# Feed-forward of a two-block kernel: weight split ahead of the conv tap, a narrower bank wait, two tiles of the second down product moved forward

## The reference, cut to what matters

```
h = rmsnorm_2(x, ffn_norm_g[l])
u = causal_dwconv(h @ w_up[l], conv_w[l], conv_b[l])
gate, val = jnp.split(u, 2, axis=-1)
x = x + (jax.nn.silu(gate) * val) @ w_down[l]
```

## Time and profile before

| | |
|---|---|
| median of 3 runs | 2674.45 us (2674.26 to 2674.68) |
| the profiled execution's own time | 2673.48 us |
| its span in the trace | 2671.7 us |
| PE busy | 2590.9 us, 97% of the span |
| DVE, ACT, POOL busy | 1443.6, 973.5, 795.2 us |
| mean granted TensorE clock | 0.993 of full |

### The profile page before, as it was taken

How to read it: one execution, slowest core, us unless ns; L and a number is a source line. 1 busy time by engine, 2 the same in 40 slices (tenths; PEclk the granted TensorE clock), 3 DMA queues, 4 the chain that set the end, 5 groups by cost and what they waited for, 6 DMA issues and landing times. The chain is left out here.

```text
span 2671.7 us, 32450 instructions
## 1 busy us (share of the span) xinstructions
PE 2590.9 (97%) x12954; PEld 2147.6 (80%) x12954; DVE 1443.6 (54%) x1290; ACT 973.5 (36%) x1380; POOL 795.2 (30%) x318
## 2 busy tenths in 40 slices
PE   7999999999999999999999999989999999999999
PEld 3788888888788888888788888877778788878887
DVE  4674546565666753444735355456866515641664
ACT  3420034435344430023556555564144302221234
POOL 2565453333443335542111011011412222222230
PEclk9999999999999999999999999999999999999999
DMA  7232221212222154241011011031111111112111
GB/s 314 73 107 69 91 84 55 61 63 64 68 71 68 48 193 139 94 142 64 32 40 40 32 40 38 34 124 51 48 39 47 48 49 46 51 51 63 47 55 63
DMA packets 55896, 194.20 MB, mean 73 GB/s; under 512 B 6584, under 2 KB 10296, under 8 KB 54624
## 3 DMA queue, kind: packets, MB, share of 16 engines
q1 hardware_dynamic: 40656, 141.61, 16.0%
q10 hardware_dynamic: 15120, 50.90, 5.4%
HBM read 158.36 MB, written 29.92 MB: 70 GB/s over the span
## 5 line engine op out<-in xcount | busy, mean ns | idle before, releaser
L238 PE MATMUL G<-H_hi,w_hi 128*128 128x512 f32 x1648 | 514.4, 393 | 7.7 <-POOL w_lo L269 4.9
L269 POOL TENSOR_TENSOR w_lo<-w_raw,w_hi 128x1024 fp32r<-128x1024 f32 x133 | 361.9, 2721 | 498.1 <-ACT w_hi L263 492.3
L238 PE MATMUL G<-H_lo,w_hi 128*128 128x512 f32 x1648 | 508.7, 390 | 0.0
L238 PE MATMUL G<-H_hi,w_lo 128*128 128x512 f32 x1648 | 508.2, 390 | 0.0
L264 POOL TENSOR_TENSOR w_hi<-w_raw,ones 128x1024 fp32r<-128x1024 f32 x75 | 195.4, 2606 | 647.0 <-PE G L238 489.9
L238 PEld LDWEIGHTS G<-H_hi,w_hi 128*128 128x128 f32 x1648 | 307.3, 188 | 73.9 <-issue 11.1
L238 PEld LDWEIGHTS G<-H_lo,w_hi 128*128 128x128 f32 x1648 | 309.9, 188 | 65.1
L238 PEld LDWEIGHTS G<-H_hi,w_lo 128*128 128x128 f32 x1648 | 309.9, 188 | 64.8
L1774 POOL TENSOR_TENSOR w_lo<-w_raw,w_hi 128x1024 fp32r<-128x1024 f32 x24 | 60.1, 2506 | 493.6 <-ACT w_hi L1983 493.6
L1824 PE MATMUL G<-A_hi,w_hi 128*128 128x512 f32 x368 | 156.9, 426 | 15.5 <-DVE projected L2166 15.2
L1876 PEld LDWEIGHTS G<-att_v,probsT 128*128 128x128 f32 x1152 | 147.9, 193 | 24.4 <-ACT probsT L2012 15.3
(11 more groups left out here) (497 smaller groups left out, 4549.1 us busy)
## 6 DMA issues: line engine op xcount, KB each, us to landing
w_raw<-w_in SPq DMA_DIRECT2D x65, 512.0 KB, 3.6
w_raw<-w_up SPq DMA_DIRECT2D x44, 512.0 KB, 3.6
pre_raw<-w_in SPq DMA_DIRECT2D x30, 512.0 KB, 3.6
w_raw<-w_out SPq DMA_DIRECT2D x16, 512.0 KB, 3.6
w_raw<-w_down SPq DMA_DIRECT2D x16, 512.0 KB, 3.6
wm<-w_mod SPq DMA_DIRECT2D x6, 1024.0 KB, 16.9
xT<-xT SPq DMA_DIRECT2D x8, 512.0 KB, 19.1
wm<-w_mod SPq DMA_DIRECT2D x2, 2048.0 KB, 24.2
```

What stands on the lines that cost most here:

```text
L238: mm = nc.tensor.matmul(dst[:, n * NB:n * NB + c], w[:, k, :], m[:, k, n * NB:n * NB + c], start=first, stop=last)
L269: nc.gpsimd.tensor_tensor(w_lo[:, slot, 0:kt, :], w_raw[:, slot, 0:kt, :], w_hi[:, slot, 0:kt, :].bitcast(F32), ALU.subtract).then_inc(w_r ...
```

## The change

Three edits in the feed-forward.

1. The first up product (job 135, `G[1]`) waits for `out2 early` number 6, the last reader of `G[1]`, and no longer for `out2 late` number 7, which reads `G[0]`. The second keeps the old wait. Both still wait for the last `out2 lo` ahead of their last k-tile.
2. `next_high` stands at the start of each half turn on ACT, ahead of the wait for `normed` and the tap.
3. In groups 0 and 1, down product 0 does all k-tiles but the last, then product 1 its first two, then product 0 its last (with the wait for `lo`), then product 1 the rest. Products 2 to 7 are as before.

```diff
@@ -2382,7 +2382,8 @@
                     if g == 0:
                         if m == 0:
                             S.wait(pe, "dve", "out2 lo", KT - 2)
-                        gemm(up + m, (up + m) % 2, H, ("dve", "out2 late", KT - 1), late=("dve", "out2 lo", KT - 1))
+                        gemm(up + m, (up + m) % 2, H, ("dve", "out2 late", KT - 1) if m else ("dve", "out2 early", KT - 2),
+                             late=("dve", "out2 lo", KT - 1))
@@ -2396,8 +2397,25 @@
                 if g < LAST:
                     S.wait(pe, "dve", f"up{g} lo", nf - 2)
-                    products_of_8(f"down{g}", down, A, nf, late=("dve", f"up{g} lo", nf - 1),
-                                  freed=[("dve", f"up{g} normed {m}", nf - 1) for m in range(2)])
+                    for m, tiles in ((0, range(nf - 1)), (1, range(2)), (0, range(nf - 1, nf)), (1, range(2, nf))):
+                        if tiles[0] == 0:
+                            pe.wait_ge(w_ready, down + m + 1)
+                            S.wait(pe, "dve", f"up{g} normed {m}", nf - 1)
+                        if tiles[-1] == nf - 1:
+                            S.wait(pe, "dve", f"up{g} lo", nf - 1)
+                        slot = (down + m) % 2
+                        for k in tiles:
+                            for w, mov in ((w_hi, A[0]), (w_hi, A[1]), (w_lo, A[0])):
+                                for n in range(2):
+                                    mm = pe.matmul(G[slot][:, halves[n]], w[:, slot, k, :], mov[:, k, halves[n]],
+                                                   start=k == 0 and w is w_hi and mov is A[0], stop=k == nf - 1 and w is w_lo)
+                        if tiles[-1] == nf - 1:
+                            mm.then_inc(gemm_done, 1)
@@ -2488,10 +2506,10 @@
                     for m in range(2):
+                        next_high(up, f, m)
                         S.wait(act, "dve", f"up{g} normed {m}", f)
                         settle(act, f)
                         tap(f"up{g}", m, f + (f0 + m * FT))
-                        next_high(up, f, m)
```

More of the change, by code:

```diff
@@ L2398, in _ @@
                     S.wait(pe, "dve", f"up{g} lo", nf - 2)
-                    products_of_8(f"down{g}", down, A, nf, late=("dve", f"up{g} lo", nf - 1),
-                                  freed=[("dve", f"up{g} normed {m}", nf - 1) for m in range(2)])
+                    for m, tiles in ((0, range(nf - 1)), (1, range(2)), (0, range(nf - 1, nf)), (1, range(2, nf))):
[12 more added lines that the diff above has]
+                            mm.then_inc(gemm_done, 1)
+                    S.enter("pe", f"down{g}")
+                    with pe.Fori(1, KT // 2) as i:
+                        for m in range(2):
+                            gemm(down + 2 * i + m, (down + m) % 2, A, ("dve", f"down{g} job {m}", i - 1), kt=nf, pair=G[(down + m) % 2])
+                    S.leave("pe", KT // 2)
             gemm(down - 2, up % 2, H, ("dve", f"up{LAST} normed 0", LAST_F - 1))
```

## The result

| | before | changed |
|---|---|---|
| median of 5 runs | 2674.45 us | 2658.86 us |
| the profiled execution's own time | 2673.48 us | 2659.00 us |
| span of it | 2671.7 us | 2657.2 us |
| PE busy | 2590.9 us | 2586.2 us |
| mean granted clock | 0.993 | 0.995 |

The changed kernel is faster: the ratio of the times is 0.9937, 95% interval 0.9921 to 0.9953. The profiled executions differ by 14.48 us, where the sum said 14.4. One execution each of the changed kernel, of the kernel before and of edits 1 and 2 without 3 took 4300 to 9000 us; ratios and ranges here leave them out, the medians contain them (without it the changed kernel's is 2657.5, and that of edits 1 and 2 is 2660.4).

What follows compares the result with a forecast made beforehand. PE was taken as the bound, losing time in four pauses. Their 1.73 + 7.80 + 2.42 + 2.47 = 14.4 us, taken from the median 2674.45, gave 2660.0 us, range 2658.9 to 2664.9.

Steps and rivals of the forecast that it cites:

- the sum: Whole kernel: 1.73 + 7.80 + 2.42 + 2.47 = 14.4 us won, profiled execution about 2659.1, median 2660.0.
- the four losses: PE pauses at first up product (1.73 us), third up product (7.80), down product 0 of groups 0 (2.42) and 1 (2.47).
- Edit 1, 1.73 us: First up product: the wait for L2283 goes, start near 1923.49, late wait costs nothing; all 1.73 us won.
- Edit 2, 7.80 us: Third up product: slab and bank ready before PE, so the 7.80 us vanish, including 2.70 at half clock.
- Edit 3, 2.42 + 2.47 us: Down products, groups 0 and 1: two k-tiles of product 1 give 2.72 us more cover; both pauses vanish.
- The step on the clock: Third up product: takes the full 2.70 us, as pairs after pauses of 2.1 to 2.8 us come at nearly full cadence.
- How the numbers follow: Whole kernel: forecast chance 0.81, own range 2659.2 to 2660.9, stated range 2658.9 to 2664.9; faster 0.95, same 0.03, slower 0.02.
- the median is 0.97 above that execution: Whole kernel: the median before, 2674.45, lies 0.97 us above the profiled 2673.48; the forecast subtracts 14.4 from the median.
- The low end of 2658.9: Whole kernel: lower end of the stated range, which runs to 2664.9 us.
- Nothing is left at the third product: Rival at the third up product: something is left, likelier 2660.5 to 2662, at worst 2667.8 us; chance 0.09.
- no down pause stayed: Rival at the down products: pauses stay, at most 2 x 2.4 us, 2664.9; chance 0.06.
- the tap is not late: Rival "Slower" in ACT's queue: tap behind the slab's load; at 10 us late the kernel near 2681; chance 0.02.

Runs made afterwards that it cites:

- the second set of runs: The changed kernel measured again with no edit: 2658.96 us against 2673.71 for the kernel before, ratio 0.9947.
- the kernel with the late split: Changed kernel with POOL's low part in the up loops of groups 1 and 2 moved behind `conv`: 2657.78 us, ratio 0.9939 to the kernel before.

## Why the prediction was right or wrong

**What bounds the kernel, and the four losses:** right. The sum of 14.4 us is 14.58 by the rest and 14.48 by the profiled executions.

**Edit 1, 1.73 us:** right. The product starts 0.46 us after the last pair of L1938, as said, and its late wait costs nothing.

**Edit 2, 7.80 us:** right, with its mechanism: slab and bank ready 4.7 and 1.4 us ahead of PE (4.4 and 1.4 said), `w_hi` at 1938.77 (1938.7 said), clock at 1.00. Not said was that edit 2 alone also takes about 3 of the 4.9 us of the down pauses; the prediction had the shorter chain and only booked it as spare room. `near` is held less than I wrote (1.65, not about 2), so the chain became 1.5 us shorter instead of 1.2. `conv` is at 1.28, as said.

**Edit 3, 2.42 + 2.47 us:** right for edit 3 alone (4.99 in the rest), and both pauses are gone. With edits 1 and 2 already in the kernel it adds only 1.9, since edit 2 has taken the other part. The total was not touched by this, since each pause is counted once in the sum.

**The step on the clock:** "at the pauses of 2.1 to 2.8 us between starts [...] the next pairs come at nearly full cadence" was read from one execution. With edit 1 alone the same pause was followed by 1.72 us of loss. For the changed kernel nothing hung on it: no pause is left there, and the 2.70 us went with the pause before them. But the sentence as a statement about pauses of that length was luck of the one execution read.

**What failed is the step "How the numbers follow", and in the sum the term "the median is 0.97 above that execution".** For the profiled execution the sum said about 2659.1, and it took 2659.00. To get a median, the prediction added the 0.97 us by which three runs of the kernel before lay above its profiled execution. In the changed kernel the median lies 0.14 us below its profiled execution. These 0.97 + 0.14 and the 0.08 by which the sum was short (14.48, not 14.4) are the whole 1.2 us between the forecast (2660.05 before rounding) and the median.

The low end of 2658.9 was built from the restarts, a remainder of 0.2 us and "some room", with no term for the scatter of executions; the three runs of the kernel before, within 0.4 us of each other, showed none. More runs did: 2655.1 to 2660.6 us for the changed kernel and 2670.1 to 2678.0 for the one before, and the medians of four sets of runs of the kernel before lie between 2673.71 and 2675.20. In the profiles this scatter is made ahead of the edits. With such a term the low end would have been near 2657. On which side of 2658.9 a median falls is chance: the second set of runs gave 2658.96, and the first without its one far execution 2657.5. Mechanism and size were right; the missing term was one of the measurement.

**The rivals:** none came. Nothing is left at the third product, no down pause stayed, and the tap is not late: in the last turn of group 0 `near`, which waits for it, starts 1.65 us after the end of `normed` (2100.87 to 2102.52), as before (2110.37 to 2112.01).

## What to carry to other kernels

When two edits shorten the same wait from both ends (one makes the late thing earlier, the other gives the waiting engine more to do), count the wait once and say what each is worth when the other is already there: here 4.9 us alone became 1.9. When a kernel's executions scatter by as much as an edit is worth, take the time from a marked instruction ahead of the edits to the end: it repeated within 0.1 us in profiles whose totals differed by 2. And give a forecast's range the scatter of executions, from more than three runs.

## What the runs showed of the hardware

A TensorE pause of 2.2 us was followed by half clock once in the six that three profiles show, at a cost of 1.7 us, and one of 8.7 us by less loss (1.9) than one of 3.2 (2.8), since the clock had fallen early in the long pause. The kernel's scatter goes with the clock too: granted clocks of 1.00, 0.97 and 0.90 in the same 50 us of unchanged code went with 107.1, 108.6 and 111.2 us for the same stretch of work. (The Trainium skill, TensorE: Matmul & The Clock Gate, section "HAM oscillation — how this bites in real kernels", ties the fall of the clock to idle gaps; the traces agree in that all eight half-clock stretches seen in the feed-forward's up and down products came with a TensorE pause of 2.2 us or more.)

POOL is held up by VectorE too. In the kernel with the late split, seven `w_lo` of group 1's loop took 3.47 to 3.48 us where the other seven took 2.40. Each of the seven started beside `act` on DVE, which has two SBUF inputs (DVE first, POOL second):

```profile
2346.16 1.23 DVE L2598 TENSOR_TENSOR A_lo<-tiles_in 128x1024 f32 x1
2346.18 3.48 POOL L269 TENSOR_TENSOR w_lo<-w_raw,w_hi 128x1024 fp32r<-128x1024 f32 x1 [8.44 <-DVE tiles_in L2577]
...
2348.88 1.86 DVE L2600 TENSOR_TENSOR A_lo<-A_lo,A_hi  x1 [1.48 <-ACT A_hi L2527]
```

`w_lo` ends 2.27 us after `act` does, and then `lo` in turn, started at 2348.88 and 1.23 us long elsewhere, ends 1.08 us after `w_lo`. In these rows whichever of the two comes second finishes as if it had begun at about the other's end.
